# A decoder block on one Trainium2 core: the second norm's rows turned by VectorE in 32x32 squares instead of by TensorE

## The reference

```python
h = rmsnorm(x, norm_mix); proj = h @ w_in          # 1024 -> 2048 columns, four parts of 512
y_lru = rg_lru(conv4(x_lru), ...) * gelu(g_lru)    # recurrent group
y_cm = silu(layernorm(conv31(v_cm * sigmoid(g_cm))))
y = concat(rmsnorm(y_lru), rmsnorm(y_cm)); x = x + y @ w_out
h = rmsnorm(x, norm_ffn)                            # "the second norm"
f = silu(h @ w_gate) * (h @ w_up)                   # 1024 -> 2816
x = x + f @ w_down
return rmsnorm(x, norm_final)
```

## Time and profile before

| | us |
|---|---|
| median of 3 runs (lowest, highest) | 1905.11 (1903.91, 1905.77) |
| span of the profiled execution | 1902.7 |
| TensorE busy, 8374 matmuls | 1875.1 |
| VectorE, ScalarE, POOL busy | 1106.6, 808.4, 1144.9 |
| DMA | 284.20 MB in 240946 packets, mean 149 GB/s |

### The profile page before, as it was taken

How to read it: one execution, slowest core, us unless ns; L and a number is a source line. 1 busy time by engine, 2 the same in 40 slices (tenths; PEclk the granted TensorE clock), 3 DMA queues, 4 the chain that set the end, 5 groups by cost and what they waited for, 6 DMA issues and landing times.

```text
span 1902.7 us, 22499 instructions
## 1 busy us (share of the span) xinstructions
PE 1875.1 (99%) x8374; PEld 1544.2 (81%) x8374; DVE 1106.6 (58%) x1269; ACT 808.4 (42%) x938; POOL 1144.9 (60%) x427
## 2 busy tenths in 40 slices
PE   9999999999999999999999999999999999999998
PEld 7888788877788788888888788888888888888886
DVE  6899988997645755455545854445443025433535
ACT  6466766585643533333333433333333222232235
POOL 3577477945734465666655755555555676676663
PEclk9999999999999999999999999999999999999999
DMA  6222132265777334533355433323333765655455
GB/s 196 78 79 88 45 100 78 75 224 172 247 240 231 117 125 127 153 119 127 112 153 176 151 105 114 106 88 105 115 105 127 288 225 190 210 189 211 166 198 221
DMA packets 240946, 284.20 MB, mean 149 GB/s; under 512 B 12095, under 2 KB 166207, under 8 KB 240364
## 3 DMA queue, kind: packets, MB, share of 16 engines
q1 hardware_dynamic: 240874, 283.25, 44.8%
q10 hardware_dynamic: 2, 0.00, 0.0%
HBM read 200.90 MB, written 82.31 MB: 149 GB/s over the span
## 4 chain that ended last, share of the span: by engine, by line
PE 82%; POOL 6%; DVE 5%; ACT 2%; issue 2%; DMA 2%; POOLq 0%; SPq 0%; DVEq 0%; ACTq 0%
PE ps L2133 19%; PE ps L2135 19%; PE ps L2134 19%; PE acc L2133 8%; PE acc L2135 8%; PE acc L2134 8%; DVE a_lo L1863 1%; POOL nsq L877 1%; PE ps L2161 1%; DVE t_sum L1887 1%; POOL nsq L879 1%; POOL w_lo L804 1%; POOL f_lo L1018 0%; DVE wo_lo L1707 0%; POOL glu L827 0%
## 5 line engine op out<-in xcount | busy, mean ns | idle before, releaser
L933 POOL TENSOR_TENSOR t_lo<-t_sum,t_hi 128x2048 fp32r<-128x2048 f32 x44 | 205.6, 4674 | 165.3 <-ACT t_hi L1366 165.2
L927 POOL TENSOR_TENSOR b_lo<-m_raw,b_hi 128x1536 fp32r<-128x1536 f32 x44 | 157.6, 3582 | 179.2 <-ACT b_hi L1361 121.9
L1018 POOL TENSOR_TENSOR f_lo<-f_raw,f_hi 128x2048 fp32r<-128x2048 f32 (+1 forms) x42 | 182.2, 4338 | 129.3 <-ACT f_hi L1518 124.8
L2133 PE MATMUL ps<-h_hi,w_hi 128*128 128x512 f32 x512 | 201.1, 393 | 0.8 <-POOL w_lo L804 0.8
L2135 PE MATMUL ps<-h_hi,w_lo 128*128 128x512 f32 x512 | 199.4, 389 | 0.0
L2134 PE MATMUL ps<-h_lo,w_hi 128*128 128x512 f32 x512 | 199.2, 389 | 0.0
L1887 DVE TENSOR_TENSOR t_sum<-m_raw 128x512 f32<-128x512 f32 x88 | 141.7, 1630 | 97.4 <-PE acc L2135 87.6
L1518 ACT CAST f_hi<-f_raw 128x2048 fp32r<-128x2048 f32 (+1 forms) x42 | 74.3, 1769 | 263.6 <-PE ps L2135 168.1
L2133 PE MATMUL ps<-wd_hi,f_hi 128*128 128x512 f32 x462 | 179.8, 389 | 0.8 <-POOL wd_lo L1025 0.8
L2134 PE MATMUL ps<-wd_lo,f_hi 128*128 128x512 f32 x462 | 179.7, 389 | 0.0
L2135 PE MATMUL ps<-wd_hi,f_lo 128*128 128x512 f32 x462 | 179.7, 389 | 0.0
(11 more groups left out here) (257 smaller groups left out, 4689.1 us busy)
## 6 DMA issues: line engine op xcount, KB each, us to landing
f_raw<-f_scr SPq DMA_DIRECT2D x35, 1024.0 KB, 4.9
wd_raw<-in_w_down SPq DMA_DIRECT2D x60, 512.0 KB, 6.6
f_scr<-fs SPq DMA_DIRECT2D x110, 256.0 KB, 2.1
m_raw<-in_w_gate SPq DMA_DIRECT2D x88, 256.0 KB, 3.9
m_raw<-in_w_up SPq DMA_DIRECT2D x88, 256.0 KB, 5.1
w_raw<-in_w_in SPq DMA_DIRECT2D x32, 512.0 KB, 5.3
f_scr<-gt SPq DMA_DIRECT2D x44, 256.0 KB, 2.0
xt<-in_x SPq DMA_DIRECT2D x16, 512.0 KB, 6.3
```

What stands on the lines that cost most here:

```text
L927: g.tensor_tensor(b_lo[b][:, :, :, :], m_raw[b][:, 0:3], f32(b_hi[b][:, :, :, :]), ALU.subtract).then_inc(s_mlo, 1)
L933: g.tensor_tensor(t_lo[b][:, :, :, :], t_sum[b][:, :, :, :], f32(t_hi[b][:, :, :, :]), ALU.subtract).then_inc(s_mlo, 1)
L1018: g.tensor_tensor(f_lo[j % 3][:, 0:n], f_raw[j % 2][:, 0:n], f32(f_hi[j % 3][:, 0:n]), ALU.subtract).then_inc(s_dlo, 1)
L2133: pe.matmul(bank, lhs[0](c), rhs[0](c), start=first, stop=False, skip_group_check=more)
```

## The change

VectorE turns the row itself, right behind `row_scaled`: one `transpose` over 128x1024, which turns each 32x32 square in its place and leaves the squares where they are. So h2t holds, at partition 32 t + j and free index (b, i), the channel 32 b + j of position 32 t + i. Four stores per row, one for each 32 partitions t, write it to a scratch whose layout is now [half, 32, 8 chunks, 4, 1024 positions]; each run in DRAM is 32 positions, 128 bytes. The loads of a quarter and of a quad are split in four as well, each into 32 partitions, with runs of 2 KB as before. TensorE's `turn_h2` and ScalarE's `h2_copy` go with all their calls. h2t gets four buffers for the first eight rows and two after that. VectorE's turn of row w waits for `row_scaled(w)` and, from row 4, for the earlier stores of its buffer. The waits on the quarter loads count four times as many completions.

```diff
-    h2_scr = nc.dram_tensor("h2_scr", [NH, P, KD, HALF], F32).ap()
+    h2_scr = nc.dram_tensor("h2_scr", [NH, SQ, KD, SQS, HALF], F32).ap()
...
-        h2t = [at(f"h2t{s}", [P, KD, P], F32, (136 + 4 * s) * KIB) for s in range(2)]
+        h2t = [at(f"h2t{s}", [P, D // SQ, SQ], F32, o * KIB) for s, o in enumerate((136, 140, 184, 188))]
...
+        def hb(w):
+            return w % 4 if w < TPH else w % 2
+        def h2_stores(n, rows):
+            return 16 * SQS * sum(hb(w) == n for w in range(rows))
...
             def store_h2(w):
                 h, i = divmod(w, TPH)
-                sp_.wait_ge(s_h2c, 2 * (w + 1))
-                sp_.dma_start(h2_scr[h, :, :, i * P:(i + 1) * P], h2t[w % 2][:, :, :]).then_inc(s_h2st[w % 2], 16)
+                sp_.wait_ge(s_turned, w + 1)
+                for t in range(SQS):
+                    sp_.dma_start(h2_scr[h, :, :, :, i * P + t * SQ:i * P + (t + 1) * SQ].rearrange("j k q s -> j (k q) s"),
+                                  h2t[hb(w)][t * SQ:(t + 1) * SQ]).then_inc(s_h2st[hb(w)], 16)
...
+            def load_quarter(n, h, a, done):
                 half, st = {"A11": (0, 0), "A12": (1, 0), "A21": (0, 1), "A22": (1, 1)}[a]
+                for q in range(SQS):
+                    sp_.dma_start(a_raw[n][q * SQ:(q + 1) * SQ],
+                                  h2_scr[h, :, half * KH:(half + 1) * KH, q, st * TILE:(st + 1) * TILE]).then_inc(done, 16)
...
-                for n, a in enumerate(("A11", "A12", "A21", "A22")):
-                    sp_.dma_start(quad[:, n], quarter(1, a)[:, k]).then_inc(s_qld, 16)
+                for n, (half, st) in enumerate(((0, 0), (1, 0), (0, 1), (1, 1))):
+                    for q in range(SQS):
+                        sp_.dma_start(quad[q * SQ:(q + 1) * SQ, n],
+                                      h2_scr[1, :, half * KH + k, q, st * TILE:(st + 1) * TILE]
+                                      ).then_inc(s_qld, 16)
...
-            def h2_copy(w):
...
-                for b in range(2):
-                    act.wait_ge(s_tr[b], w + 1)
-                    a.copy(h2t[w % 2][:, 4 * b:4 * b + 4], ps[6 + b].rearrange("p (k s) -> p k s", k=4)
-                           ).then_inc(s_h2c, 1)
...
+            def row_turned(w):
+                dve.wait_ge(s_hn, w + 1)
+                if w >= 4:
+                    dve.wait_ge(s_h2st[hb(w)], h2_stores(hb(w), w))
+                v.transpose(h2t[hb(w)].rearrange("p b i -> p (b i)"), hn[w % 2][:, :]).then_inc(s_turned, 1)
...
                 if w == 3:
+                    row_turned(0)
+                    row_turned(1)
                     row_scaled(2)
                 if w == 1 or 3 <= w < NT - 2:
                     row_scaled(w)
+                if w == 3:
+                    row_turned(2)
+                if 3 <= w < NT - 2:
+                    row_turned(w)
...
                 sum12(m, i, b, h, first)
                 sum22(m, i, b, h, first)
+                if first and not b:
+                    row_turned(NT - 2)
+                    row_turned(NT - 1)
...
-            def turn_h2(w):
-                pe.wait_ge(s_hn, w + 1)
...
-                    for k in range(4):
-                        c = (4 * b + k) * P
-                        mm = pe.transpose(ps[6 + b][:, k * P:(k + 1) * P], hn[w % 2][:, c:c + P], ident[:, :])
-                    mm.then_inc(s_tr[b], 1)
```

More of the change, by code:

```diff
@@ L50, in hybrid_block @@
     HD = gate_a_w.shape[2]
+    SQ = 32
+    SQS = P // SQ
     PAD4, PAD31 = TAPS4 - 1, TAPS31 - 1
@@ L301, in hybrid_block @@
         s_xr = [sem(f"residual_loaded{n}") for n in range(4)]
-        s_tr = [sem(f"turned{b}") for b in range(2)]
         s_std2 = sem("std2_ready")
         s_hn = sem("hn_ready")
-        s_h2c = sem("h2_copied")
-        s_h2st = [sem(f"h2_stored{n}") for n in range(2)]
+        s_turned = sem("hn_squares_turned")
+        s_h2st = [sem(f"h2_stored{n}") for n in range(4)]
         s_x2st = [sem(f"x2_stored{n}") for n in range(2)]
@@ L647, in _ @@
                 if w == LOAD_AT:
-                    for n in range(2):
-                        sp_.wait_ge(s_h2st[n], 16 * TPH // 2)
+                    for n in range(4):
+                        sp_.wait_ge(s_h2st[n], h2_stores(n, TPH))
                     sp_.wait_ge(s_out[3], TPH)
@@ L653, in _ @@
                     for n, a in (((6, "A22"), (5, "A21")), ((1, "A11"), (0, "A12")))[w - LOAD_AT]:
-                        sp_.dma_start(a_raw[n][:, :, :], quarter(0, a)).then_inc(s_a0, 16)
+                        load_quarter(n, 0, a, s_a0)
                 if w == LOAD_AT + 2:
@@ L703, in _ @@
                     if i == QUADS[0]:
-                        for n in range(2):
-                            sp_.wait_ge(s_h2st[n], 16 * NT // 2)
+                        for n in range(4):
+                            sp_.wait_ge(s_h2st[n], h2_stores(n, NT))
                     if i - 1 in QUADS:
@@ L725, in _ @@
                         sp_.wait_ge(s_pr[n], MH)
-                        source = {0: quarter(1, "A12"), 1: quarter(1, "A11"), 6: quarter(1, "A22")}.get(n)
-                        sp_.dma_start(a_raw[n][:, :, :], hs_scr[n - 2] if source is None else source
-                                      ).then_inc(s_ald[n], 16)
+                        source = {0: "A12", 1: "A11", 6: "A22"}.get(n)
+                        if source is None:
+                            sp_.dma_start(a_raw[n][:, :, :], hs_scr[n - 2]).then_inc(s_ald[n], 16)
+                        else:
+                            load_quarter(n, 1, source, s_ald[n])
                         if n == 4:
@@ L1108, in norm_rms_cm, with norm_swish @@
                 a.activation(rms[:, 8 * m + 1:8 * m + 8:2], ps[bank][:, 0:4], ACT.Sqrt, bias=eps[:, 0:1]).then_inc(s_rsts, 1)
-            def norm_swish(m, between=None, turned=None):
+            def norm_swish(m, between=None):
                 act.wait_ge(s_dn, m + 1)
@@ L1117, in norm_swish @@
                     y_split(between)
-                if turned is not None:
-                    h2_copy(turned)
                 act.wait_ge(s_ysw, NJ * (m + 1))
@@ L1374, in _ @@
                     row_std(1)
-                    norm_swish(1, between=DIRECT[1], turned=0)
-                    h2_copy(1)
+                    norm_swish(1, between=DIRECT[1])
                 if 4 <= w < NT - 1:
@@ L1458, in second_a_high @@
             def second_a_high(n):
-                act.wait_ge(s_ald[n], 16)
+                act.wait_ge(s_ald[n], 16 * (SQS if n in (0, 1, 6) else 1))
                 a_high(n)
@@ L1482, in gate_block @@
                 sums_hi(m + 1, 1)
-                if starts == 0:
-                    h2_copy(NT - 1)
                 silu(i, 1, h)
@@ L1870, in first_half_sum @@
                 if n == 0:
-                    dve.wait_ge(s_a0, 64)
+                    dve.wait_ge(s_a0, 64 * SQS)
                 else:
@@ L2370, in _ @@
                     norm_var(1, 6)
-                for turned in TURNED.get(w, (w - 1,) if 5 <= w < NT - 1 else ()):
-                    turn_h2(turned)
             BANKS = [[ps[4], ps[5], ps[0], ps[5], ps[0], ps[5], ps[5]], [ps[4], ps[1], ps[0], ps[1], ps[0], ps[1], ps[1]]]
```

25 lines of the change are left out of this document (3 added, 22 removed).

## The result

The changed kernel takes 1921.87 us (median of 4 runs, 1917.9 to 1926.27) beside 1904.55 us of the kernel before: a ratio of 1.0088, 95% interval [1.0069, 1.0106]. Beside the experiments it was 1920.24 beside 1905.96, ratio 1.0071 [1.0059, 1.0083]. So it is slower, as forecast, but by 14 to 17 us where I had 5.1. The profiled execution took 1926.27 us, the longest of the four, with a span of 1924.5. Two executions beside the experiments, one of the kernel before (3165.87 us) and one of experiment 6 (3176.32 us), ran at a granted clock of 0.56 and are left out of all ratios.

What follows compares the result with a forecast made beforehand. TensorE, busy 1875.1 of 1902.7 us, was taken as the bound. Terms -11.2 + 9 + 1.3 + 4.0 + 2 = +5.1 gave a 1907.8 us span, forecast as 1910.2 us; range 1898 to 1930, or 1905 to 1916 for the forecast alone.

Steps and rivals of the forecast that it cites:

- -5.0: Turns after rows 3 and 4 leave TensorE, a 0.52 us wait goes, POOL's folds follow: 5.0 us saved.
- +2.0: Second half: three split quarters at the change of halves cost 2 us (0 to 4); the quads cost 0.
- The turn on VectorE: Each 128x1024 turn on VectorE takes 1.25 us (ends 0.6 and 2.5), hidden in ordinary rows but not at row 12.
- The quarters: Each quarter load, split into 32 partitions, takes 4.4 us instead of 2.75, so 1.65 more.
- Row 13: Rows 9 to 12: y lands 8 us later, VectorE's sums and first eviction also late; +9 us.
- Matrix 2: Its load stands behind the longer stores of rows 14 and 15 on SP, delaying TensorE's fourth product: +4.0 us.
- A: Rival: transfers stay hidden, split loads run at full pace, short packets cost 12 ns; 1898.7 us, chance 0.30.
- B: Rival: small DRAM stores cost 28.6 ns or more a packet; waits already in rows 5 to 8; 1932 us, chance 0.17.
- C: Rival: VectorE becomes the bound, a turn taking 2.5 us and getting in POOL's way; 1915 us, chance 0.08.
- the clock, "+1.3": After row 13's new wait the granted clock drops to 1.2 GHz for half of 5 us: +1.3 us.
- the stores of rows 3 to 7: Four small-packet stores there cost some 8 us, counted only within rival B.
- gain of 11.2: Turns leaving TensorE save 5.0 us after rows 3 and 4 and 6.2 after rows 8 to 14.

Runs made afterwards that it cites:

- experiment 6: Kernel before, with matrix 2 loaded ahead of the stores of rows 14 and 15: 1906.3 us, ratio 0.9997.
- experiment 4: Kernel before, with only each load of a quarter or quad split into four of 32 partitions: 1915.36 us, ratio 1.0053.
- experiment 5: Changed kernel, with the loads of matrices 2 and 3 ahead of the stores of rows 14 and 15 on SyncE: 1912.9 us, ratio 1.0033.
- experiment 9: Changed kernel, with turns of a constant square on TensorE ahead of five waits, about as long as each: 1914.98 us, ratio 1.0054.
- turn only: Changed kernel, with one 512-byte-run store a row and whole 128-partition loads, squares not put in place: 1900.04 us, ratio 0.9964.
- experiment 10: Changed kernel again, unaltered, beside the other experiments (gives "its second profile"): 1920.24 us, ratio 1.0071.
- experiment 11: Changed kernel, whole loads, matrix 2 loaded earlier, VectorE turning rows 11 and 12 later, ScalarE splitting row 14's y earlier: 1899.13 us, ratio 0.9963.
- experiment 12: Experiment 11's kernel, with turns of a constant square on TensorE ahead of four waits: 1900.79 us, ratio 0.9972.
- wide stores: Changed kernel, with one 512-byte-run store a row, loads still split, squares not put in place (also "with split loads"): 1909.18 us, ratio 1.0011.
- idle turns: Changed kernel, with eight constant-square turns on TensorE in every place of an old turn, nobody waiting for them: 1920.88 us, ratio 1.0079.
- whole loads: Changed kernel, with each quarter or quad loaded by one DMA into 128 partitions (also "with small stores"): 1907.81 us, ratio 1.0004.

## Why the prediction was right in sign and low in size

TensorE's timeline gives the starts of rows 2, 8 and 13 (the first of 16 matmuls on wo_hi, y_hi) and of the first product of matrices 0 and 2. The stretches between them, less those of the kernel before (84.4, 60.9, 34.6, 44.7 and 1233.9 us), beside my terms:

| stretch | forecast | profile above | its second profile |
|---|---|---|---|
| up to row 2 | 0 | -0.9 | +1.2 |
| row 2 to row 8 | -5.0 | +3.0 | -1.8 |
| row 8 to row 13 | -4.4 + 9 = +4.6 | +5.7 | +5.8 |
| row 13 to matrix 0 | -1.8 + 1.3 = -0.5 | +0.1 | +0.2 |
| matrix 0 to matrix 2 | +4.0 | +7.7 | +7.9 |
| from there to the end | +2.0 | +6.1 | +5.3 |
| sum | +5.1 | +21.7 | +18.6 |

Both executions are slower than their medians, by 4.4 and 2.9 us (1926.27 and 1923.11 against 1921.87 and 1920.24), so the typical sum is 14 to 17. The 84.4 us of the kernel before are at the low end too: experiments 6 and 4, with its code up to row 8, took 86.3 and 86.7.

**Right.** *The turn on VectorE*, 1.24 us. *The quarters*: 4.6 us for 4.4. *Row 13*: the y 9.7 us late (I had 8), the sums 9 us later, a wait of 7.24 and the term of +9 minus turns met within 1.2 us. The closeness is partly luck: a drop of the clock behind row 8, which the term did not have, is in it. Where that drop is missing (experiments 5 and 9) row 8 to row 13 takes 63.8 and 64.0 us, 2.9 and 3.1 more than before where I had 4.6 and both profiles 5.7 and 5.8. The mechanism is shown by the same stretch in the other kernels: 58.7 us in turn only, 59.6 with small stores, 62.6 with split loads, and 65.5 against 60.9 for split loads without the turn. So it is mostly the width of the loads, 3.9 to 4.6 us where the small stores alone cost 0.9. *Matrix 2*: the product on y2s starts 38.7 us behind matrix 0 (38.9 in experiment 10), before 33.8: 4.9 late for 4.0. (The wait of 3.52 ahead of it is no loss of the transfers. It is the 2.63 of the earlier trace rows plus the 0.88 us of a row's turns, which I had put at 0; turn only has it too, 3.51.) Experiments 5 and 6 show it is SyncE's order with the longer stores: eight issues from 657.15 on, and VectorE waiting for the matrix until 669.44:

```profile
657.15 5.68 SPq L560 DMA_DIRECT2D h_scr<-h2t  x8
...
669.44 0.69 DVE L1884 TENSOR_TENSOR t_sum<-m_raw 128x512 f32<-128x512 f32 x1 [11.19 <-DMA m_raw<-in_w_gate]
```

*The rivals.* A fell with the DMA share (1.05 over 560 to 600) and experiment 4. B's price fell with the 11.8 ns, but its sign, waits in rows 5 to 8, was there (below). C fell with the 1.24 us. The Trainium skill (DMA: Bandwidth & Descriptors, Specifications) asks for 512 bytes or more to reach line rate and names a read-modify-write below that. The trace agrees on the rate (179 GB/s, against 286 by the 28.6 ns of 512-byte packets), but no packet is dearer than the longer ones, whose rows gave 17.7 and 28.6 ns; no run here shows the read-modify-write itself.

**Too small: the clock, "+1.3".** I priced one drop of the clock, behind row 13, by the row at 1073.41 and gave it half of 2.5 us. In the changed kernel one stands behind each of the six waits quoted above. (It is no law: in the kernel before the wait of 2.63 us had none behind it.) What they cost can be read where a twin lacks the drop:

| | with a drop | without |
|---|---|---|
| row 8 to row 9 | 14.7, 14.8 (both profiles) | 12.0, 11.9 (experiments 5, 9) |
| row 13 to row 14 | 12.9, 13.0 | 10.9 (row 14 to row 15) |
| product on y2s to matrix 2 | 13.7, 13.7 | 10.9 (kernel before) |
| matrix 0 to matrix 2, a drop behind the first wait only | 44.7 (experiments 4, 6, 11) | 44.7 (kernel before, experiment 12) |

The first three cost 2.8, 2.1 and 2.8 us, 7.7 in all where I had 1.3. The fourth costs nothing, though its window at 0.64 lists 2.9: TensorE waits for other operands behind it anyway. So the stretch of matrices 0 and 1 closes: 4.9 us late, 2.8 of slow work behind, 7.7 measured. Over whole runs the mean granted clock is 0.996 (median) in the kernel before and 0.989 in the changed one on the same chip: 7.6 and 21.1 us of full-speed time. Of those 13.5 us only a part is time lost. Experiment 9, at 0.994, gives back 9.6 us of clock and 3 to 6 of time; a drop that falls while TensorE would wait anyway is free. Row 3 shows that: VectorE is done with the same instructions at 457.92 in both traces, and TensorE waits 0.63 us before and 3.87 in the changed kernel. Windows 443 to 451, first of before, then of the changed kernel:

```profile
443.00:451.00 8.00, 8.00 (x22) 5.72 (x23) 7.75 (x9) 5.52 (x9) 6.12 (x3) 0.60 0.16 66
```
```profile
443.00:451.00 8.00, 8.00 (x35) 6.26 (x35) 7.73 (x9) 5.47 (x9) 6.12 (x3) 1.00 0.16 66
```

In the first a slow stretch took the time in which TensorE would have waited; in the second it waited and had its slow stretch afterwards. So row 3's wait is not the change's doing: it was 0.57 us in experiment 10 and 3.87 in experiment 4, the kernel before up to there.

**Wrong: the stores of rows 3 to 7, not in the sum.** I priced them only within rival B (some 8 us) and gave the forecast nothing; waits in rows 5 to 8 were my sign for B. They came, at less than B's price: row 5 to row 8 takes 40.8 us before, 40.2 in turn only and in wide stores, and 45.4 and 45.2 in the two profiles of the changed kernel. In the other kernels with small stores it is 43.9 to 45.1, but for idle turns (41.0), which come to row 5 later. So small stores cost 3.7 to 5.2 us here. Windows 480 to 520 of before, of turn only and of whole loads:

```profile
480.00:520.00 40.00, 39.09 (x189) 31.40 (x187) 25.05 (x24) 24.19 (x31) 28.09 (x14) 1.00 0.82 272
```
```profile
480.00:520.00 40.00, 40.00 (x179) 32.01 (x177) 27.93 (x26) 21.67 (x26) 26.90 (x14) 1.00 0.85 281
```
```profile
480.00:520.00 40.00, 36.91 (x165) 29.07 (x163) 24.69 (x22) 21.20 (x25) 22.81 (x13) 1.00 1.01 253
```

The share goes from 0.85 to 1.01 by the small stores alone. The y of row 7 is then late. ScalarE's split of it in the turn-only kernel, in whole loads and in the changed kernel:

```profile
501.23 1.03 ACT L1271 CAST y_hi<-y_raw 128x1024 fp32r<-128x1024 f32 x1
```
```profile
504.20 1.05 ACT L1273 CAST y_hi<-y_raw 128x1024 fp32r<-128x1024 f32 x1 [3.47 <-DMA y_raw<-d_scr]
```
```profile
509.02 1.06 ACT L1276 CAST y_hi<-y_raw 128x1024 fp32r<-128x1024 f32 x1 [5.02 <-DMA y_raw<-d_scr]
```

On ScalarE the swish and squares stand behind that split, on POOL the folds behind the squares and the y_lo of row 8 behind the folds: one late load, and TensorE waits 2.49 us before row 7, not at all in turn only, and everything behind moves. (The 3.07 before row 8 are not new: turn only has 2.87 there.) So the 5.0 of the early turns was gained (turn only reaches row 8 in 79.3 us, 5.1 less) and mostly given back. Part of the +3.0 of the first profile is scatter, as experiment 4 shows: it takes 2.3 us more to row 8 than the earlier trace rows's execution with the same code.

**Too high: the gain of 11.2.** The turn alone brought 6 to 7 us. In its profile matrix 0 starts 7.0 us earlier than before and matrix 2 5.7; of the 4.4 us of five turns between rows 8 and 13 only 2.2 arrive (58.7 us for 60.9), for row 8 starts after a wait of 2.87 us on POOL's y_lo and the granted clock is 0.96 over 520 to 560. Behind it rows 13, 14 and 15 wait 0.47, 1.76 and 0.20 us on a row eviction and y_lo, so of the 1.8 us of two more turns nothing arrives at matrix 0. The two moves of experiment 11 go at these waits, and with them the kernel with its squares in place reaches the ratio of turn only (0.9963).

**Open.** From matrix 2 to the end the changed kernel lost 5 to 6 us, 3 to 4 over my +2. The other kernels took 1233.3 to 1237.4 us there, the kernel before with matrix 2 first among them, so 3 us of this is scatter. The traces narrow the rest down to the waits around the change of halves. TensorE's in the kernel before (beside the 2.40 of the earlier trace rows) and in the changed one:

```profile
1062.57 0.47 PE L2133 MATMUL ps<-a_hi,b_hi 128*128 128x512 f32 x1 [1.55 <-ACT p5s L1448]
```
```profile
1061.84 0.50 PE L2146 MATMUL ps<-a_hi,b_hi 128*128 128x512 f32 x1 [4.50 <-ACT p5s L1448]
...
1094.10 0.77 PE L2146 MATMUL acc<-a_hi,t_hi 128*128 128x512 f32 x1 [3.08 <-DVE gt L1969]
```

Every kernel with whole loads waits 3.6 to 4.0 us in these places, every one with split loads 5.0 to 7.6 (a wait on y2s, which comes and goes without regard to the change, left out). So split loads cost 1 to 3.6 us there, with slow clock behind; whether by the quads or by the three quarters was not taken apart.

## What to carry to other kernels

A layout that saves compute can cost transfers at both ends: price a DMA by the partitions it spans and the packets it makes, and charge it in every stage where the DMA share is near 1, not only in the busiest one. To a new wait of several us on TensorE's path add 2 to 3 us of slow clock behind it, unless TensorE waits again soon after, and look what else stands behind a late load in the queue of each engine. When the work of one engine shrinks, reread the hand-written order: here whole loads, matrix 2 ahead and two small moves made the difference between +0.7% and -0.4%.

## What the hardware did that I had not expected

- A store of 128-byte packets is cheap per packet, 11.8 ns (179 GB/s), but four of them can hold SyncE for 10.40 us while the DMA engines are full.
- After waits of 2.5 to 7.2 us the granted clock was 0.50 to 0.68 over the next 4 to 8 us, whatever the length of the wait: the window behind 7.24 us lost 2.2 us of full-speed work, that behind 3.87 lost 3.3. Behind 2.65 us (experiment 6) it was 0.79 over 8 us, behind 2.63 (kernel before) 1.00.
- A load into 32 partitions moved 226 GB/s where one into 128 moved 393, with the same 2 KB packets.
- The price of an added wait depends on what the clock does next to it: 56 idle squares ahead of a 7 us wait kept the clock at 1.00 and, with the other four fills, very likely made the whole somewhat faster; the same trick ahead of waits of 1 to 3.5 us brought nothing.
